# Two FFNs by seven products in a two-layer trunk: gated rows left in PSUM, a wait of the A22 copy moved, memory sums on GpSimd, squares of last rows added a row later

## What is computed

```python
def swiglu(x, w_in, w_out):
    a, b = jnp.split(x @ w_in, 2, axis=-1)
    return (jax.nn.silu(a) * b) @ w_out

for l in range(DEPTH):
    h = h + 0.5 * swiglu(rmsnorm(h, ffn1_norm[l]), ffn1_w_in[l], ffn1_w_out[l])
    u = rmsnorm(h, mix_norm[l])
    ... u @ w_in[l]; sparse attention, pooling mixer,
    y_c = mem_attention(q_c, rmsnorm(mem, mem_norm[l]), w_mem_kv[l])
    ... h = h + merged @ w_out[l]
    h = h + 0.5 * swiglu(rmsnorm(h, ffn2_norm[l]), ffn2_w_in[l], ffn2_w_out[l])
return rmsnorm(h, final_norm)
```

## Time and profile before

| | us |
|---|---|
| median of 3 runs (2213.0 to 2216.5) | 2215.24 |
| the profiled execution | 2214.67 |
| its span in the profile | 2212.9 |
| TensorE matmuls busy | 2141.6 (97%) |
| TensorE weight loads busy | 1928.8 (87%) |
| VectorE busy | 1678.9 (76%) |
| GpSimd busy | 1490.8 (67%) |
| ScalarE busy | 1068.6 (48%) |

### The profile page before, as it was taken

One profiled execution on the slowest core, in us unless ns is written; L12 is line 12 of the kernel. 1 busy time (PEld: TensorE's weight loads), 2 busy tenths in 40 slices (PEclk: granted clock), 3 DMA queues, 4 the chain that ended last, 5 costly groups with the idle time before them and its releaser, 6 DMA issues. The chain is left out here.

```text
span 2212.9 us, 39425 instructions
## 1 busy us (share of the span) xinstructions
PE 2141.6 (97%) x13990; PEld 1928.8 (87%) x13990; DVE 1678.9 (76%) x3116; ACT 1068.6 (48%) x2067; POOL 1490.8 (67%) x1094
## 2 busy tenths in 40 slices
PE   9999998999999999999999999989999999999997
PEld 6999997788888889999879999968788888999996
DVE  6888887568765588888778888865787555888884
ACT  5545542444554255564345455434445533555552
POOL 6877866544445678788768788765444466788874
PEclk9999999999999999999999999999999999999999
DMA  5332333322222323333323233332222133232232
GB/s 167 108 109 92 115 106 110 116 70 67 72 63 77 106 85 101 107 99 101 109 82 117 96 101 114 109 121 93 69 63 72 54 108 96 81 111 97 98 104 85
DMA packets 95235, 213.18 MB, mean 96 GB/s; under 512 B 10400, under 2 KB 13640, under 8 KB 94792
## 3 DMA queue, kind: packets, MB, share of 16 engines
q1 hardware_dynamic: 90864, 205.42, 28.7%
q10 hardware_dynamic: 4184, 5.31, 0.7%
HBM read 208.58 MB, written 3.68 MB: 96 GB/s over the span
## 5 line engine op out<-in xcount | busy, mean ns | idle before, releaser
L791 POOL TENSOR_SCALAR wH<-raw 128x1024 fp32r<-128x1024 f32 (+2 forms) x184 | 173.4, 942 | 422.3 <-PE bank L921 352.3
L794 POOL TENSOR_TENSOR wL<-raw,wH 128x1024 fp32r<-128x1024 f32 (+2 forms) x184 | 389.1, 2115 | 15.3
L1051 PE MATMUL bank<-u1H,wH 128*128 128x256 f32 x1152 | 330.8, 287 | 10.3 <-DVE far4L L2031 6.3
L1052 PE MATMUL bank<-u1H,wL 128*128 128x256 f32 x1152 | 327.1, 284 | 0.0
L1053 PE MATMUL bank<-u1L,wH 128*128 128x256 f32 x1152 | 327.0, 284 | 0.0
L836 POOL TENSOR_TENSOR wL<-wS,wH 128x512 fp32r<-128x512 f32 x208 | 273.1, 1319 | 74.3 <-ACT wH L1497 39.3
L836 POOL TENSOR_TENSOR wL<-raw,wH 128x512 fp32r<-128x512 f32 x208 | 280.5, 1369 | 2.2 <-ACT wH L1503 2.1
L919 PE MATMUL bank<-u1H,wH 128*128 128x512 f32 x704 | 281.6, 400 | 0.0
L920 PE MATMUL bank<-u1H,wL 128*128 128x512 f32 x704 | 275.0, 391 | 0.0
L921 PE MATMUL bank<-u1L,wH 128*128 128x512 f32 x704 | 274.8, 390 | 0.0
L1051 PE MATMUL bank<-u0H,wH 128*128 128x256 f32 x864 | 248.3, 287 | 9.4 <-DVE ta L1959 9.1
(11 more groups left out here) (332 smaller groups left out, 6113.4 us busy)
## 6 DMA issues: line engine op xcount, KB each, us to landing
raw<-in_wA SPq DMA_DIRECT2D x296, 256.0 KB, 2.9
raw<-in_wM SPq DMA_DIRECT2D x96, 512.0 KB, 3.5
raw<-in_wO SPq DMA_DIRECT2D x128, 256.0 KB, 2.9
raw<-in_wA SPq DMA_DIRECT2D x28, 512.0 KB, 3.6
raw<-in_wC SPq DMA_DIRECT2D x32, 384.0 KB, 3.0
raw<-in_wR SPq DMA_DIRECT2D x32, 256.0 KB, 2.6
keep<-in_memT SPq DMA_DIRECT2D x4, 512.0 KB, 3.3
mem<-in_memT SPq DMA_DIRECT2D x2, 1024.0 KB, 7.5
```

The lines of the kernel that those rows point to most:

```text
L791: pool.tensor_scalar(wH[:, w, 0:cols], raw[:, slot, 0:cols], 1.0, 0.0, ALU.mult, ALU.add).then_inc(rounded, 1)
L794: pool.tensor_tensor(wL[:, w, 0:cols], raw[:, slot, 0:cols], wH[:, w, 0:cols].bitcast(F32), ALU.subtract).then_inc(split_done, 1)
L1051: pe.matmul(dst, a, hi, start=begin and k == 0, stop=False)
L1052: pe.matmul(dst, b, hi, start=False, stop=False)
```

## The change

- `copy_a22` waits for the A22 low of the pair before (`late_low` at 2(g-1)+1), no longer for its S4 low.
- Gated rows of groups A and B no longer go to `keep`: an S pair's stays in `obank`, a K pair's in `bank[2]`. High, low and couple sums read them there. For a near row, ScalarE first copies the whole row to `sumS`, then rounds from that copy.
- Couple sums: a far row's cross sums become one operation over both halves, then a half one; three sums per couple are counted in place of four. For K pairs they stand ahead of the S4 low, for S pairs behind it.
- Banks 2 and 3 change places: S1 and S3 go to 3, A22 and S4 to 2. Product A22 waits for the couple sums of the pair before. Banks 2 and 3 are allocated as one tensor, and `finish_blocks` makes two of its half sums in one operation that reads both banks. `mix_first` makes both halves in one, into `obank`; ScalarE copies the crossing half back (`copy_cross`).
- `add_mem` moves from VectorE to GpSimd, after `k_weights` two pairs later.
- `last_row` adds the square of the row before while it waits for its own high. The memory root and `norm_mem` stand after the second row, the memory highs after the third, the memory lows after the fourth. The normalised factor is left in `obank`.

The core of the diff (declarations of the tensors and semaphores, and helpers with the new counts, are left out):

```diff
@@ GpSimd
+                def add_mem(p):
+                    k = 4 * N_GROUP[p.group] + p.at
+                    pool.wait_ge(mem_squared, l * KD + k + 1)
...
+                    pool.wait_ge(mem_ssq, l * KD + k)
+                    pool.tensor_tensor(mem_rms[:, :], mem_piece[:, p.at, :], mem_rms[:, :], ALU.add
+                                       ).then_inc(mem_ssq, 1)
@@ TensorE, seven_products
+                        bank_free(p, 3)
+                        pe.wait_ge(pool_low, pool_lows_to(g, "S1"))
+                        product(bank[3][:, low], g, "S1", lambda k: sum_of(p, k, 1), begin=True)
+                        product(bank[3][:, high], g, "S3", lambda k: sum_of(p, k, 3), end=True)
                         bank_free(p, 2)
...
+                        before = FLOW[p.pos - 1]
+                        if before.kind == "K" and in_couple(before):
+                            pe.wait_ge(couple_sum, summed(ffn_at(l, f), before))
                         pe.wait_ge(late_low, 2 * g + 1)
...
+                        product(bank[2][:, low], g, "A22", lambda k: sum_of(p, k, 4), begin=True)
@@ ScalarE
                     def copy_a22(p):
                         g = k_at(l, f, p)
                         act.wait_ge(quarter_landed["A22"], 16 * (g + 1))
-                        act.wait_ge(late_low, 2 * g)
+                        if g:
+                            act.wait_ge(late_low, 2 * (g - 1) + 1)
...
+                    def copy_cross(p):
+                        act.wait_ge(mixed, k_at(l, f, p) + 1)
+                        act.activation(ta[:, TH:T], obank[:, TH:T], ACT.Copy).then_inc(cross_copied, 1)
...
+                        src = made_in(p)[:, :]
+                        if in_couple(p) and p.at < 4:
+                            act.activation(sumS[:, 2 * p.at, :], src, ACT.Copy).then_inc(first_kept, 1)
+                            act.wait_ge(first_kept, couple_at(ffn_at(l, f), p) + 1)
+                            src = sumS[:, 2 * p.at, 0:TH]
+                        act.activation(hi, src, ACT.Copy).then_inc(k_high if p.kind == "K" else hidden_high, 1)
...
                         if seven_then:
                             round_s2(then)
+                        if seven_now:
+                            copy_cross(now)
+                        if seven_then:
                             round_sum(then, "S1")
...
-                    if k == 0:
+                    if k == 1:
                         root(l * 5 + 2, mem_rms[:, :], M)
-                    if k == 1:
+                    if k == 2:
                         act.wait_ge(mem_normed, l + 1)
@@ VectorE
-                        own.done(dve.tensor_tensor(obank[:, 0:TH], bank[1][:, 0:TH], ta[:, 0:TH], ALU.add))
-                        dve.tensor_tensor(ta[:, TH:T], bank[1][:, TH:T], ta[:, 0:TH], ALU.add).then_inc(mixed, 1)
+                        dve.tensor_tensor(halves(obank[:, :]), halves(bank[1][:, :]), twice(ta[:, 0:TH]), ALU.add
+                                          ).then_inc(mixed, 1)
...
-                        own.done(dve.tensor_tensor(bank[3][:, 0:TH], bank[3][:, 0:TH], sg[:, 1, TH:T], ALU.add))
...
-                        dve.tensor_tensor(bank[3][:, TH:T], bank[2][:, 0:TH], sg[:, 1, TH:T], ALU.add
+                        dve.tensor_tensor(halves(bank[2][:, :]), banks_two[:, :, 0:TH], twice(sg[:, 1, TH:T]), ALU.add
                                           ).then_inc(crossed, 1)
...
+                            dve.wait_ge(first_kept, c + 1)
+                            dve.tensor_tensor(near[:, left], made[:, right], near[:, left], ALU.subtract
                                               ).then_inc(couple_sum, 1)
                             return
+                        dve.wait_ge(couple_sum, 3 * c + 1)
+                        dve.tensor_tensor(halves(cross), twice(made[:, right]), halves(near), ALU.subtract
                                           ).then_inc(couple_sum, 1)
+                        dve.wait_ge(couple_sum, 3 * c + 2)
+                        dve.tensor_tensor(near[:, right], made[:, left], cross[:, left], ALU.subtract
                                           ).then_inc(couple_sum, 1)
...
                             low(last)
+                        if last is not None and last.kind == "K" and in_couple(last):
+                            couple_sums(last)
                         if seven_now:
                             low_late(now, "S4")
...
+                    dve.scalar_tensor_tensor(ps, ps, 0.5, h[:, k, :], ALU.mult, ALU.add).then_inc(h_added, 1)
+                    if k:
+                        add_square(k - 1, n - 1)
...
-                    if k == 0:
+                    if k == 1:
                         norm_mem()
-                    if k == 1:
+                    if k == 3:
                         low_mem()
```

More of the change, by code:

```diff
@@ L482, in gain @@
             return pr[:, bass.ds(at + k, 1)]
[L486 removed]
+        bank = [ctx.enter_context(nc.psum_tensor(f"bank{i}", [P, 512], F32)) for i in range(BANKS - 2)]
+        banks_two = ctx.enter_context(nc.psum_tensor("banks_two", [P, 2, 512], F32))
+        bank += [banks_two[:, i, :] for i in range(2)]
         sbank = [ctx.enter_context(nc.psum_tensor(f"sbank{i}", [P, 512], F32)) for i in range(2)]
@@ L875, in ffn_units @@
                         before = FLOW[p.pos - 2] if p.pos >= 2 else None
-                        if before is not None and in_couple(before) and before.at >= 4:
+                        if before is not None and second_of(before):
                             couple_lows(f, before)
+                        if before is not None and before.kind == "O" and f == 0:
+                            add_mem(before)
                     first = u_first[f] + OUT_UNIT
@@ L1835, in inverse_rms @@
                 own.wait()
-                own.done(dve.scalar_tensor_tensor(dst, mean, 1.5, dst, ALU.add, ALU.mult))
+                own.done(dve.scalar_tensor_tensor(dst if into is None else into, mean, 1.5, dst, ALU.add, ALU.mult))
                 own.wait()
@@ L1964, in mix_two @@
                         dve.wait_ge(product_done, 7 * g + 5)
-                        dve.wait_ge(mixed, g + 1)
+                        dve.wait_ge(cross_copied, g + 1)
                         dve.wait_ge(crossed, g)
-                        dve.tensor_tensor(halves(sg[:, 1, :]), halves(bank[2][:, :]), twice(ta[:, TH:T]), ALU.add
+                        dve.tensor_tensor(halves(sg[:, 1, :]), halves(bank[3][:, :]), twice(ta[:, TH:T]), ALU.add
                                           ).then_inc(mixed_two, 1)
@@ L1974, in finish_blocks @@
                         dve.wait_ge(mixed_two, g + 1)
-                        own.done(dve.tensor_tensor(obank[:, TH:T], bank[3][:, TH:T], sg[:, 1, 0:TH], ALU.add))
-                        own.done(dve.tensor_tensor(bank[3][:, 0:TH], bank[3][:, 0:TH], sg[:, 1, TH:T], ALU.add))
+                        own.done(dve.tensor_tensor(obank[:, TH:T], bank[2][:, TH:T], sg[:, 1, 0:TH], ALU.add))
                         own.wait()
@@ L1988, in add_rows @@
                         dve.wait_ge(crossed, g + 1)
-                        own.done(dve.tensor_tensor(bank[3][:, :], bank[3][:, :], rms[:, :], ALU.mult))
+                        own.done(dve.tensor_tensor(bank[2][:, :], bank[2][:, :], rms[:, :], ALU.mult))
                         own.wait()
-                        for i, made in ((0, obank), (1, bank[3])):
+                        for i, made in ((0, obank), (1, bank[2])):
                             row = h[:, 2 * p.at + i, :]
@@ L2078, in window @@
                             scale_first(now)
+                        if last is not None and last.kind == "S":
+                            couple_sums(last)
                         if seven_then:
```

97 lines of the change are left out of this document (47 added, 50 removed).

## The result

The kernel after takes 2153.66 us (median of 4 runs, 2152.95 to 2154.11), the kernel before, run beside it, 2214.12. The ratio of after to before is 0.973, 95% interval 0.9711 to 0.975. The forecast was 2147 in 2134 to 2172: 60.5 us of gain where 68 were worked out. The profiled run took 2153.76 us, its span 2151.7.

What follows compares the result with a forecast made beforehand. Late VectorE was taken to hold up TensorE in hidden stages and output rows. Gains of 48.7 (stages), 16.6 (output rows) and 3.6 us (rows after FFN 2) make 68.9; 2215.2 less 68 is 2147, range 2134 to 2172.

Steps and rivals of the forecast that it cites:

- TensorE's least time and the losses by stage: Hidden stages: 262.1 us at best each, 59 us lost in all four, 48.7 of it to be gained.
- A22 copy: Hidden stages: ScalarE's copy runs beside VectorE's low, giving back about 0.75 us per pair, some 19 us of VectorE per stage.
- Gated rows and joined sums: Couples: PSUM rows save some 2 us per couple, less 1.3 of new waiting; joined block sums 0.13 each, twice per pair.
- Memory sums: Output pairs: eight operations of at most 1.32 us move to GpSimd, which has room in a 262 us stage; free.
- Output rows: Output rows with the memory part, both layers: loss falls from 15.5 to 7.0 us in each, 16.6 us gained.
- Lows to 374.1: Output rows: the memory lows, after row 4's high frees its bank at 371.0, end at 374.1; rows 5 to 8 follow.
- Rows after FFN 2: Layer 1's rows after its second FFN: the 2.23 us eighth-row wait and half-level clock go, 3.6 of 3.8 us gained.
- VectorE stays the bound in couples: Rival, couple pairs: new ScalarE steps aren't covered, a couple costs 21.7 us; at half of that 2166 us; chance 0.18.
- The output rows give nothing: Rival, output rows: lost time moves to the memory units, the 16.6 us stay, 2164 us; chance 0.08.
- the three waits: Output rows: TensorE waits 0.9 us for bank 3, 1.8 at the first memory unit and 2.6 at the third.
- The bank 2 loop: Slower rival, couple pairs: product 6 waits for the sums, VectorE for product 7; 3 us more each gives 2238; chance 0.04.

Runs made afterwards that it cites:

- the kernel with the late sums: Kernel after with the couple sums of K pairs put back at the end of VectorE's window, behind `mix_two`: 2328.63 us.

## Why the prediction was right, and where not

The mechanism was right in the stages, and one term was wrong in the output rows. That the number is off by only 7 us is in part luck: the stages gave 4.5 us more than worked out and the two output parts 10.9 less. (The terms add up to 68.9 us, and 68 were taken off.)

- *TensorE's least time and the losses by stage.* Right: VectorE no longer holds it, and the stages came to 1.0 us over the least. The first was given 6.5 us of loss and has 2.9. Its three waits at the start sum to 2.6 us, the longest 1.5 rather than 2.73, and the half-level clock behind it didn't come (granted 1.00). That term was 3.6 us too dear, and is most of the 4.5 by which the stages beat the forecast.
- *A22 copy.* Right: ScalarE waited 51.9 us for VectorE in a stage and now 7.3; the copy ends 4.9 us into the pair (forecast 5.1) and `sum_two` starts at 6.4. The 18 to 20 us that this idle time holds in a stage aren't its price, though. Alone the edit gives at most 13.8 in one, and as the last of the edits 8.6 in all four.
- *Gated rows and joined sums.* Right. The new waiting was charged at 1.3 us for two pairs and is 1.1, but of another make: 0.58 us at the near row's high, none at the far one, and 0.26 in each pair for the sigmoid, which the forecast didn't name. Two pairs agree with the sum to 0.1 us.
- *Memory sums.* "Free" on GpSimd held. What the move was worth came out as 0.4 us without the other edits and 4.8 with them, a single run each.
- *Output rows.* The step that failed is "Lows to 374.1". The 16.6 us for two layers became 3.3 + 2.4 = 5.7. Rows 1 and 2 came early, the eight multiplications fell from 6.26 us to 2.74, the highs held row 4's low for 3.19 us, rows 5 to 8 stand 2.78 us apart, all as worked out. But the lows were priced as if nothing ran beside them. The price of their swelling stood in the earlier trace rows, where such operations cost 0.6 to 1.1 us extra, and was applied only to those that the change removes, not to the eight that it moves beside GpSimd's splits. The 3.1 us were the price of the old place, where GpSimd was idle. With 9.1 us in the sum row 5 starts 6 us later, and the schedule gives TensorE 7.8 rather than 1.8 us at the first unit: 7.5 were measured. The run with one input in PSUM shows no other term far off: with lows of 3.2 us the two parts, read from stage to stage, are 9.1 + 8.6 = 17.7 us shorter than before, where 16.6 were worked out.
- *Rows after FFN 2.* 4.2 us against 3.6; no wait, clock 1.00.
- *Rivals.* "VectorE stays the bound in couples" fell: it waits for TensorE in both pairs. "The output rows give nothing" was the nearest to the truth in its part, by another mechanism than the three waits it leant on. The bank 2 loop was put at 9.0 us against 10.08, and is 5.9 + 2.9 + 0.1 = 8.9. With the sums 4.0 us later it gives 12.9, 2.8 more than a pair, and the clock costs 0.9 besides: the forecast's price had left the clock out.

The kernel after with the lows behind the seventh row beats both kernels: 2142.2 us, 3.2% less than before (with the highs spread as well it is no faster). It gains 11.4 us on the kernel after by the medians and 10.5 between the profiled runs. Of these, 5.4 lie in the output rows of layer 1 (56.96 against 51.60) and 4.5 in those of layer 2.

## What to carry to other kernels

Before you move an operation, look at what the other engines run at the new place, and price it by its inputs: here one that reads two SBUF tensors cost, beside a GpSimd that works through large tiles, up to the whole length of a GpSimd instruction (2.6 us rather than 0.47), and one with an input in PSUM cost what it does elsewhere. A duration read at the old place holds only if the neighbours are the same. Where several edits relieve the same engine, their prices from the idle rows don't add up: subtract until that engine falls below the one it holds up, and stop. A buffer handed from one engine to another and back is a loop, and its length against the pair is one sum, which should be made for the order that is planned and for the one it replaces.

## What the runs showed of the hardware

An operation of VectorE with two SBUF inputs doesn't slow down in proportion beside GpSimd, it is held until GpSimd's instruction ends. The eight lows of after one by one, from the trace: the first, at 351.92, met a rounding (351.95 to 353.00) and took 1.35; the second started at 353.19, when a subtraction of GpSimd (353.08 to 355.52) had just begun, and ended at 355.80; the three that began between that and the next rounding took 0.47 each; one that met the rounding (356.60 to 357.89) took 1.25, one that met the next subtraction 2.56, and the last, behind it, 0.47. Each of the four that were held ends 0.3 us after GpSimd's instruction. An operation with one input in PSUM (346.02, the add to h) took its 0.69 us beside an earlier subtraction (344.93 to 347.33), and in the run with the lows' input in PSUM none of the eight took more than 0.48. The Trainium skill, "SBUF — State Buffer" (SBUF: two separate sides), states just this, that whichever starts first gets the pair "for the whole instruction; the other fully blocks", and the trace agrees on the hold. GpSimd's side fits it too: the rounding that began at 356.60, while a low was running (356.51 to 356.99), took 1.29 us rather than 1.05. Who started first can't be read from the recorded starts: the first low has a start 0.03 us ahead of the rounding's, and was the one that was held. GpSimd's rounding, with one SBUF input, holds VectorE as its subtraction does.

The fixed cost of a PSUM input, 62 cycles more than for SBUF in "VectorE: DVE Perf Modes" (the TRN2 errata) of the Trainium skill, isn't seen in this operation: the same low took 475 ns with its first input in PSUM and 476 with it in SBUF. The measurement decides.

In the kernel with the late sums a wait of TensorE of 2.6 us cost 3.7 on average, 0.9 of it by the half-level clock that followed 27 of the 48 waits: 17 of the 24 of about 2.85 us and 10 of the 24 shorter ones, of 2.3 to 2.6. The three waits of 0.4 to 1.5 us in the first stage of after were followed by none.
